# Where VectorE's share of the modulation stands, and who makes layer 1's gate, in a four-layer fp32 kernel

## What is computed

```python
shift, scale, gate = split(silu(c) @ mod_w[i] + mod_b[i], 3)       # latent; c_ctx gives the same for context
h_lat = rms_norm(x, norm_g[i]) * (1 + scale) + shift               # h_ctx alike
y_lat, y_ctx = mixer(h_lat, h_ctx)                                  # ... @ w_out
x = x + gate * y_lat;  ctx = ctx + cgate * y_ctx                    # ctx not in the last layer of a network
```

## Time and profile before

| | |
|---|---|
| median of 3 runs | 2962.39 us (2959.8, 2962.39, 2965.26) |
| profiled execution | 2953.81 us, span 2952.1 us, mean granted TensorE clock 0.966 |
| TensorE busy | 2737.0 us, 93% |
| VectorE busy | 1838.1 us, 62% |
| ScalarE busy | 1212.8 us, 41% |
| GpSimd busy | 361.5 us, 12% |
| moved by DMA | 488.85 MB, mean 166 GB/s |

### The profile page before, as it was taken

One profiled execution on the slowest core, in us unless ns is written; L12 is line 12 of the kernel. 1 busy time (PEld: TensorE's weight loads), 2 busy tenths in 40 slices (PEclk: granted clock), 3 DMA queues, 4 the chain that ended last, 5 costly groups with the idle time before them and its releaser, 6 DMA issues.

```text
span 2952.1 us, 42367 instructions
## 1 busy us (share of the span) xinstructions
PE 2737.0 (93%) x14546; PEld 2203.6 (75%) x14546; DVE 1838.1 (62%) x2660; ACT 1212.8 (41%) x1859; POOL 361.5 (12%) x485
## 2 busy tenths in 40 slices
PE   5899999898899999999989899999997996889989
PEld 1477777687577777777779577888885776888879
DVE  4599999997664655546464533344545886665654
ACT  3355555422444443444444422333444224443652
POOL 1110110253200000000013200000000442110000
PEclk8799999999999999999999999999999996899999
DMA  9755555475455545445535453322122663674325
GB/s 371 305 163 161 174 175 160 161 228 181 156 192 179 183 174 185 171 172 188 180 119 180 148 199 112 97 86 88 69 72 90 205 212 99 227 240 137 123 92 170
DMA packets 118628, 488.85 MB, mean 166 GB/s; under 512 B 13584, under 2 KB 15632, under 8 KB 103440
## 3 DMA queue, kind: packets, MB, share of 16 engines
q1 hardware_dynamic: 74176, 267.49, 26.6%
q0 software_dynamic: 44368, 220.22, 22.0%
HBM read 485.56 MB, written 2.10 MB: 165 GB/s over the span
## 4 chain that ended last, share of the span: by engine, by line
PE 66%; DVE 16%; issue 8%; DMA 6%; ACT 3%; DVEq 1%; POOL 0%; POOLq 0%; ACTq 0%; SPq 0%
PE psum L247 17%; PE psum L249 17%; PE psum L248 17%; DVE w_lo L229 4%; DVE psum L334 3%; PE psum L261 3%; DMA y<-in_mod_weights 2%; DMA work<-in_mod_units 2%; DVE work L336 2%; DVE h_lo L443 1%; PE psum L901 1%; PE psum L1418 1%; DMA modraw<-in_mod_units 1%; PE psum L944 1%; ACT w_hi L221 1%
## 5 line engine op out<-in xcount | busy, mean ns | idle before, releaser
L247 PE MATMUL psum<-h_hi,w_hi 128*128 128x512 f32 (+1 forms) x3840 | 1372.8, 357 | 80.3 <-DVE h_lo L443 40.6
L249 PE MATMUL psum<-h_hi,w_lo 128*128 128x512 f32 (+1 forms) x3840 | 1335.3, 348 | 0.0
L248 PE MATMUL psum<-h_lo,w_hi 128*128 128x512 f32 (+1 forms) x3840 | 1335.0, 348 | 0.0
L229 DVE TENSOR_TENSOR w_lo<-raw,w_hi 128x1024 fp32r<-128x1024 f32 x496 | 590.6, 1232 | 606.1 <-ACT w_hi L221 605.0
L247 PEld LDWEIGHTS psum<-h_hi,w_hi 128*128 128x128 f32 x3840 | 736.9, 192 | 202.5 <-issue 41.5
L248 PEld LDWEIGHTS psum<-h_lo,w_hi 128*128 128x128 f32 x3840 | 737.9, 192 | 94.8 <-issue 10.0
L249 PEld LDWEIGHTS psum<-h_hi,w_lo 128*128 128x128 f32 x3840 | 737.1, 192 | 89.8
L221 ACT ACTIVATE w_hi<-raw 128x1024 fp32r<-128x1024 f32 x496 | 496.6, 1051 | 334.4 <-PE psum L249 323.5
L334 DVE SCALAR_TENSOR_TENSOR psum<-work,modraw 128x1024 f32<-128x1024 f32 x128 | 182.4, 1425 | 10.5 <-DMA work<-in_mod_units 10.5
L336 DVE SCALAR_TENSOR_TENSOR work<-work,modraw 128x1024 f32<-128x1024 f32 x128 | 165.7, 1295 | 0.0
L267 POOL DMA_DIRECT2D modraw<-in_mod_weights x80 | 42.6, 533 | 809.6 <-PE psum L261 800.1
(11 more groups left out here) (254 smaller groups left out, 2739.6 us busy)
## 6 DMA issues: line engine op xcount, KB each, us to landing
raw<-in_weights SPq DMA_DIRECT2D x496, 512.0 KB, 4.5
modraw<-in_mod_weights POOLq DMA_DIRECT2D x96, 1024.0 KB, 5.2
work<-in_mod_units POOLq DMA_DIRECT2D x128, 512.0 KB, 4.4
y<-in_mod_weights POOLq DMA_DIRECT2D x16, 1024.0 KB, 8.9
modraw<-in_mod_units POOLq DMA_DIRECT2D x32, 512.0 KB, 4.8
modraw<-in_cond_rows POOLq DMA_DIRECT2D x4, 1024.0 KB, 6.2
work<-in_gate_w POOLq DMA_DIRECT2D x16, 256.0 KB, 5.1
work<-in_x_t POOLq DMA_DIRECT2D x16, 256.0 KB, 3.3
```

Source lines behind the costliest of these rows:

```text
L229: dve.tensor_tensor(w_lo[:, par, half, :], raw[:, 2 * par + half, :], w_hi[:, par, half, :].bitcast(F32), ALU.subtract).then_inc(S["split_ ...
L247: pe.matmul(dst, hi, h_hi[:, k, 0:n], start=(k == 0), stop=False)
L248: pe.matmul(dst, hi, h_lo[:, k, 0:n], start=False, stop=False)
L249: mm = pe.matmul(dst, lo, h_hi[:, k, 0:n], start=False, stop=(k == KT - 1))
```

## The change

1. **Layer 1's gate.** Groups run in heads 0 to 11 alone (the gate's four groups are dropped, layer 2's twelve stay). In heads 12 to 15, now written out, VectorE makes the gate's 16 x 128 columns for the latent condition with `unit_lat`, four units per head, one behind each of the four splits. A condition row (1 MB) is loaded, tanh and silu taken, ahead of head 12; POOL loads these units.
2. **End of layer 0's mixer.** Unit 31 moves from the last block to behind tile 0 of layer 0's output stage, and `mod_a` is made behind it; so POOL's first additions wait for it. The load of unit 32 is issued by `out_pool` behind its first tile.
3. **Output stages' units** follow a plan, counted per pair as (tile 0, tile 1). Layer 0: 2 and 2 in pair 0 (unit 31 among them), 1 and 1 in pairs 1 to 3, 2 and 1 in pair 4, 1 and 1 in pairs 5 and 6, none in pair 7. Layer 2: none in pair 0, 2 and 2 in pair 1, 1 and 1 in pairs 2 and 3, 2 and 2 in pair 4, 1 and 1 in pairs 5 and 6, none in pair 7.
4. **Layer 2's output stage**, POOL: context tiles are fetched ahead of the condition rows, and the first pair's additions and fetches are queued ahead of the wait for the silu.
5. **Layer 3's SGU**: half a unit behind each of the three splits and behind L1275; loads one unit earlier.
6. **Start**: feature tiles 0 to 11 of the first two strips, interleaved, are multiplied four at a time behind each pair of modulation groups; the last four follow in the mixer.

The core of the diff (a line of "..." marks what is left out):

```diff
-M_SGU = M_ATT + HEADS1
+ATT_MODS = 12
+M_SGU = M_ATT + ATT_MODS
-AT_ATT, AT_SGU = 20, 40
+AT_ATT, AT_SGU = 24, 40
+U_ATT = U_OUT0 + KT
+U_OUT2 = U_ATT + KT
...
+        def unit_lat(dve, p, half, slot):
+
+            dve.wait_ge(unit_in[half], 16 * (MOD_FIRST + p + 1))
+            dve.scalar_tensor_tensor(out=mw_sgu[:, half, :], in0=mw_sgu[:, half, :], scalar=0.5, in1=cb[:, 0, half * 1024:(half + 1) * 1024],
+                                     op0=ALU.mult, op1=ALU.mult, accum_out=macc[:, 0, 0, half:half + 1]).then_inc(S["unit_used"], 1)
+            if half == 1:
...
+        UNIT_PLAN = {0: [(0, 1, 2, 2), (1, 4, 1, 1), (4, 5, 2, 1), (5, 6, 1, 1), (6, 7, 1, 1), (7, 8, 0, 0)],
+                     1: [(0, 1, 0, 0), (1, 7, 0, 0), (7, 8, 0, 0)],
+                     2: [(0, 1, 0, 0), (1, 2, 2, 2), (2, 4, 1, 1), (4, 5, 2, 2), (5, 6, 1, 1), (6, 7, 1, 1), (7, 8, 0, 0)],
+                     3: [(0, 7, 0, 0), (7, 8, 0, 0)]}
...
-                if l == 2:
-                    cb_load(pool, 1)
                 for c in range(2):
                     fetch(c, c, True)
                 if l == 2:
-                    pool.wait_ge(S["cond_ready"], 9)
-                    unit_load(pool, U_OUT2, mw_work)
+                    cb_load(pool, 2)
...
+                def pair(j, units):
+                    begin, end = (isinstance(j, int) and j == n for n in (0, KT // 2 - 1))
                     for c in range(2):
+                        add(2 * j + c, c, begin and c == 0)
+                        if l in fetched and not end:
                             fetch(2 * j + 2 + c, c, False)
+                        for p in units(j, c):
+                            if not (isinstance(p, int) and p + 1 in (U_ATT, U_SGU)):
+                                unit_load(pool, p + 1, mw_work)
+                    if begin and l == 2:
+                        pool.wait_ge(S["cond_ready"], 11)
+                        unit_load(pool, U_OUT2, mw_work)
...
+            def pair(j, units):
+                end = isinstance(j, int) and j == KT // 2 - 1
                 for c in range(2):
+                    tile(j, c, end and (l == 3 or c == 1))
+                    for p in units(j, c):
+                        if isinstance(p, int) and p == U_OUT0 - 1:
+                            unit(dve, p, c, 4 * KT + KT - 1)
+                            dve.wait_ge(S["unit_cols"], U_OUT0)
+                            next_scale()
+                        else:
+                            unit(dve, p, c, p + (KT if l == 0 else 5 * KT), 0 if l == 0 else KT)
...
-            unit_load(pool, U_OUT0, mw_work)
+
+        def first_tiles(pe, k0, k1):
+
+            for k in range(k0, k1):
+                half, kk = divmod(k, HALF)
+                pe.wait_ge(S["h_ready"], k + 1)
+                for c in range(2):
...
+            def first_block():
+                first_tiles(pe, KT - 4, KT)
+                gates(0, 0)
...
-                unit(dve, 2 * b + 1, 1, 3 * KT + SCALE + b)
+                if not last:
+                    unit(dve, 2 * b + 1, 1, 3 * KT + SCALE + b)
...
-            pool.wait_ge(S["unit_used"], 2 * U_OUT2)
-            with pool.Fori(0, HEADS1) as i:
+            pool.wait_ge(S["unit_used"], 2 * U_ATT)
+            with pool.Fori(0, ATT_MODS) as i:
                 for q in range(4):
                     mod_load(pool, M_ATT + i, q)
+            pool.wait_ge(S["mod_used"], 4 * M_SGU)
+            cb_load(pool, 1)
+            pool.wait_ge(S["cond_ready"], 7)
+            with pool.Fori(U_ATT, U_OUT2) as p:
+                unit_load(pool, p, mw_sgu)
...
+            def light(i, n):
+
+                if isinstance(i, int) and i >= ATT_MODS:
+                    for half in range(2):
+                        unit_lat(dve, U_ATT + 4 * (i - ATT_MODS) + n, half, 3 * KT + GATE + 4 * (i - ATT_MODS) + n)
...
+                if isinstance(i, int) and i == ATT_MODS:
+                    cb_silu(dve, 1, mw_sgu)
                 if here:
                     next_strip(split_lo, dve, att_strip(j, par, 0))
+                    light(i, 0)
...
                     next_strip(split_lo, dve, att_strip(j, par, 3))
+                    light(i, 3)
...
                     next_strip(split_lo, dve, sgu_strip(lay, j, par, 0))
+                    light(i, 0)
...
-                    if lay == 1:
-                        for u in range(2):
-                            unit_lat(dve, U_SGU + 2 * i + u, u, 9 * KT + GATE + 2 * i + u)
+                    light(i, 3)
...
-            with pe.Fori(1, MOD_FIRST // 2) as j:
+            for j in range(1, MOD_FIRST // 2):
                 for par in range(2):
                     products(2 * j + par, par)
                     mod_turn(pe, 2 * j + par - 1, 0, first_bank[1 - par])
-            mod_turn(pe, MOD_FIRST - 1, 0, first_bank[1])
+                if j == MOD_FIRST // 2 - 1:
+                    mod_turn(pe, MOD_FIRST - 1, 0, first_bank[1])
+                first_tiles(pe, 4 * (j - 1), 4 * j)
```

More of the change, by code:

```diff
@@ L269, in mod_chunk @@
         def mod_chunk(pe, m, q):
[L270 removed]
+            loads = 2 if isinstance(m, int) and m >= M_SGU and q % 2 == 0 else 1
+            pe.wait_ge(modraw_in[q % 2], 16 * (2 * (m - MOD_FIRST) + q // 2 + 1 + loads))
             if q == 0:
@@ new lines, in build, with unit_plan, of @@
+        UNIT_PLAN = {0: [(0, 1, 2, 2), (1, 4, 1, 1), (4, 5, 2, 1), (5, 6, 1, 1), (6, 7, 1, 1), (7, 8, 0, 0)],
[3 rows of a table added]
+        def unit_plan(l):
+            at = {0: U_OUT0 - 1, 2: U_OUT2}.get(l, 0)
+            for j0, j1, *per in UNIT_PLAN[l]:
+                each, first = sum(per), at
+                def of(j, c, j0=j0, per=per, each=each, first=first):
+                    return [each * j + (first - each * j0 + (per[0] if c else 0) + n) for n in range(per[c])]
+                yield range(j0, j1), of
+                at += each * (j1 - j0)
@@ L355, in normalize_bufs, with out_loop @@
+        def out_loop(eng, l, body):
+            for js, of in unit_plan(l):
+                if len(js) == 1:
+                    body(js[0], of)
+                else:
+                    with eng.Fori(js[0], js[-1] + 1) as j:
+                        body(j, of)
         def normalize_bufs(space):
@@ L627, in out_dve, with tile @@
                     op0=ALU.add, op1=ALU.mult).then_inc(S["mod_a_done"], 1)
-            def tile(j, c, last, first=False):
+            if l in (1, 2):
+                next_scale()
+            def tile(j, c, last):
                 st = Strip(out_strip[l], c, j)
@@ L690, in lru_pool, with gates @@
                     block(2 * j + par, par, False)
-            unit_load(pool, U_OUT0, mw_work)
+        def first_tiles(pe, k0, k1):
[3 more added lines that the diff above has]
+                for c in range(2):
+                    if kk == 0:
+                        pe.wait_ge(S["split_lo"], 2 * c + half + 1)
+                    hi, lo = (w[:, c, half, kk * P:(kk + 1) * P] for w in (w_hi, w_lo))
+                    pe.matmul(psum[:, c, :], hi, h_hi[:, k, :], start=(k == 0), stop=False)
+                    pe.matmul(psum[:, c, :], hi, h_lo[:, k, :], start=False, stop=False)
+                    mm = pe.matmul(psum[:, c, :], lo, h_hi[:, k, :], start=False, stop=(k == KT - 1))
+                    if k == KT - 1:
+                        mm.then_inc(S["strip_done"], 1)
         def lru_pe(pe):
-            def block(j, par, first=False):
+            def gates(j, par):
                 b = 2 * j + par
-                su, sg = Strip(S_LRU, 2 * par, j, 4), Strip(S_LRU, 2 * par + 1, j, 4)
-                ge(pe, L["u_evac"], b)
-                strip(pe, su, psum[:, U_BANK, :], NT,
-                      operand=(S["h_ready"], 0) if first else None)
-                ge(pe, L["silu_done"], b)
-                strip(pe, sg, psum[:, G_BANK, :], NT)
                 pe.wait_ge(L["xc_ready"], b + 1)
@@ L1149, in sgu_pool @@
                         table(2 * j + 2 + par, par, False)
-                for g in range(GROUPS - 2, GROUPS):
-                    units(g)
+                units(GROUPS - 2)
+                unit_load(pool, N_UNITS - 1, mw_sgu)
         def sgu_pe(pe, lay):
```

156 lines of the change are left out of this document (76 added, 80 removed).

## The result

The kernel after takes 2946.42 us (median of 5 runs, 2939.03 to 2947.64), the kernel before 2962.39 us (5 runs): ratio 0.9935, 95% interval 0.9917 to 0.9953. That is 16.0 us less, where 22.4 were forecast; the time lies 6.4 us above the forecast one and inside the range. The profiled execution took 2947.43 us.

A forecast was written before the change was run, and what follows sets the result against it. TensorE is busy 93% of the span, but what holds it up differs by stage. The stage terms sum to -22.4 us: 2931.4 us in the profile's time, 2940.0 in the median's; range 2922 to 2958.

The forecast's parts named there:

- heads 12 to 15: Layer 1: gate units on VectorE delay ScalarE's root, keys and queries; each head 3.4 us longer, +17.0 us in all.
- the bound: Layer 1's heads 12 to 15: upper limit of +24 us, if half clock after each gap is not absorbed.
- Layer 3's SGU stage: Half units behind each split end the waits for loads; seven groups at 18.8 instead of 23.76 us, -34.7 us.
- Rival 4: Layer 3's SGU stage: halves land late, needing 280 GB/s; the whole 34.7 us is lost, 2974.7 us, slower; 5%.
- Ends of stages 0 and 2: Output stages of layers 0 and 2: without units there, TensorE's waits before the row sums go; -9.3 and -9.6 us.
- First pair: Layer 0's output stage: unit 32's late load makes TensorE wait 7.9 and 3.8 us, plus half clock; +15.3 us.
- pair 4: Layer 0's output stage: three units find VectorE 3 to 4 us behind with 8.8 allowed; +0.5 us.
- Mixer's end: Layer 0: unit 31 leaves VectorE's path, TensorE's 2.09 us wait for h_lo and its half clock go; -3.8 us.
- Layer 2's stage: Output stage: earlier context fetches give -8.3 us; four units in pair 4 cost waits of 3.0 and 4.4, +10.9 us.
- Start: First two strips interleaved with modulation groups: TensorE gains 11.1 us, but VectorE's chain sets the pace; -0.4 us.
- Rival 3: Doubled units and heads cost their upper bounds (+20, +4, +13, +24): 15 us more, 2955 us, no change; 8%.
- The gain of 19 us: Heads 12 to 15 of layer 1: units all hidden on VectorE, TensorE relieved, -19.2 us, 2903.8 us; a rival, 7%.

The follow-up runs named there:

- a_sgu: Kernel after with layer 3's half units all behind the group's last step again, loads still one unit earlier: 2979.78 us, 1.0062 of the kernel before.
- a_pair0: Kernel after with unit 31 back in the mixer, layer 0's output stage at one unit per tile, extras at tiles 8 and 14: 2934.68 us, 0.9913 of before.
- a_pair1: Kernel after, unit 31 left in place, one unit per tile in layer 0's pair 0, displaced units in pair 6 and at tile 14: 2944.88 us, 0.9940 of before.
- a_gate: Kernel after with layer 1's gate made on TensorE again, no units in heads 12 to 15: 2926.02 us, 0.9877 of the kernel before.
- a_idle: Kernel after with all eight half units of each of heads 12 to 15 placed where VectorE idled: 2921.01 us, 0.9872 of the kernel before.
- best_tail: Kernel after with start undone, unit 31 back, output plans eased, gate halves in VectorE's idle slots, last two units in layer 1's output stage: 2899.22 us, 0.9786 of before.

## Why the prediction was right, and where it was off

Right in sign and within the range; the likeliest time was 6.4 us too low. Some of this is luck. The sum was made in the time of the profile, and there it missed by 16.0 us (2931.4 forecast, 2947.43 measured). In the table's first columns these 16.0 are 7.0 in the heads, 5.6 at the start, 5.1 in stages that nothing changed, and -1.7 in the rest. The first profile of before lay 8.6 us below its median and that of after 1.0 above its own, so the medians hide 9.6 of them.

The step that failed most is the sum of **heads 12 to 15**: the half clock behind the ssk wait was left to the bound.

- **Layer 3's SGU stage**, -34.7: measured -34.9 and -35.3. The mechanism (units in a row that wait for their load, ahead of a split) and the size were right, and a_sgu shows it. Rival 4 asked for 280 GB/s; the stage moves 284, and VectorE waits for a half only once, 0.93 us in the first group.
- **Ends of stages 0 and 2**, -9.3 and -9.6: -10.1 and -9.5 from the last strip to the next layer's first. No run undoes this part alone. A unit at tile 14 leaves no wait ahead of the row sums in a_pair0, and 4.37 us in a_pair1, where one unit more stands ahead of it.
- **First pair**, +15.3 (and +0.5 for pair 4): the stage from the first evacuation to the last strip is 15.2 us longer. That the size fits is partly luck: the first wait was 6.4 instead of 7.9 (the half unit landed 3.8 us after its issue and not 4.8, which is 1.0 of it), so some 5.0 us beside the two waits stand where 3.6 of half clock were forecast. The granted clock was 0.50 for 3.6 us behind the first wait. a_pair1 shows that the wait works through the order of VectorE's queue, as the prediction put it.
- **Mixer's end**, -3.8: -3.3.
- **Layer 2's stage**, -8.3 and +10.9: -7.5 and +8.2. Pair 4's two waits are 1.5 and 5.8 us where I had 3.0 and 4.4: their sum was right, but behind the shorter one the clock stayed at 1.00, so its half clock was counted too high. No run undoes the new order of GpSimd's fetches; the -7.5 is read from the profiles alone.
- **Heads**, +17.0: +24.0 and +19.9. The ssk wait has the forecast place and size (5.1; 4.93 to 4.99 measured). The wait for the keys (L922) is at most 0.9 us where 0.6 to 2.1 were forecast, that for the queries (L937) 1.4 to 2.5 instead of 1.0. But heads follow at 53.4, 50.7 and 52.6 us in one profile and 52.9, 50.4 and 50.7 in the other, where I had 50.4. What I left to the bound ("half clock after each gap not absorbed") is there in every head: the granted clock between ssk matmuls is 0.92 to 0.97, against 1.00 in a_gate, and TensorE is busy for 43.2 to 46.0 us with matmuls that take 41.4 at full clock in a_idle. Those 1.8 to 4.6 us per head are the missed term. A gap of 5 us has to be priced with its half clock, as I did in the output stages and did here only for one of the waits.
- **Start**, -0.4: the two profiles of after lie 4.6 and 5.2 us above the first of before up to the end of the mixer, 2.6 to 3.2 above the second, and over all profiles the difference is 2 us within a scatter of 9. I had put 5 us of matmuls ahead of the products of groups 4 and 5 and forgotten a second batch of 24 ahead of the last two; together 11 us of work ahead of the last turn, which came 6.9 us later than in the first profile of before.
- **Stages with no change** moved by up to 4 us between two profiles of one kernel. Against a single profile of before that was among its fastest executions, a sum cannot be checked; the stages can.
- **Rival 3** has a slip in its sum: the upper bounds that it names add up to 17.3 us more, not 15, so its time was 2957. It changes neither the forecast nor the range.

The trace also answers the rule of the Trainium skill (Perfetto Trace Analysis, Identifying the Most-Contended Engine) that I set against the rows. It names TensorE as the engine to relieve here; the section has TensorE judged by MFU and the busy share of its weight loads rather than by its matmuls, and at 77% the loads stand above VectorE's 56% as well. The gain of 19 us was my own step from there. The heads lost 20 to 24 us where the units stood and broke even where a_idle put them. The rule names the engine, the order of the queue of the one that takes the work over sets the price.

## What to carry to other kernels

Before work is moved to an engine that idles half of the time, list its idle slots against what is queued behind each: the same eight half units per head cost the stretch 20 to 24 us or nothing against the gate on TensorE. Behind every gap of TensorE of about 5 us add the half clock, and ask of each load behind a single buffer what else its queue will hold up. Compare stages, not spans, when two profiles of one kernel differ by more than the change.

## What was unexpected of the hardware

- TensorE's granted clock fell from 2.4 to 1.2 GHz for eight matmuls in a stretch with nothing new ahead of them, in one execution and not in another: 1.6 us. Six steps of 1.3 to 2.4 us lie between two profiles of the kernel before; that all of them are falls of the clock was looked up for this one only.
- Waits of 2.3 us once per head did or did not cost clock: in a_idle the mean between two ssk matmuls was 1.00, 0.97 and 1.00 (43.8, 45.2 and 43.7 us for the same work), in best_tail 0.96, 0.96 and 1.00. With waits of 5.0 us it was 0.92 to 0.97 each time.
